# DeltaNet norms by 32-column sums and 32-row spreads, and adaLN units of a spot summed in one bank

## What is computed

```python
mod = silu(c) @ ada_w[l] + ada_b[l]          # once for the context's c_ctx, once for the latents' c
h = rmsnorm(x, norms[0]) * (1 + scale1) + shift1
z = h @ w_in                                 # attention, gMLP and DeltaNet inputs, gates
q = l2norm(silu(short_conv(q))) * DK ** -0.5 # l2norm(x) = x * rsqrt(sum(x * x) + EPS), 4 heads of DK = 128
k = l2norm(silu(short_conv(k)))
merged = g_a * (o_a @ wb[0]) + g_b * (o_b @ wb[1]) + g_c * (o_c @ wb[2])
x = x + gate1 * rmsnorm(merged @ w_out, norms[1])
h2 = rmsnorm(x, norms[2]) * (1 + scale2) + shift2
x = x + gate2 * rmsnorm(ffn(h2), norms[3])   # layer 0: dense SwiGLU; layer 1: top 2 of 8 experts
```

## Time and profile before

| | before |
|---|---|
| median of 3 runs | 2011.56 us (2010.69 to 2015.3) |
| the profiled execution's own time | 2011.39 us |
| its span, first to last instruction | 2009.5 us |
| PE busy | 1895.5 us (94%) |
| PE weight loads busy (beside PE) | 1658.8 us (83%) |
| DVE busy | 1174.5 us (58%) |
| ACT busy | 948.3 us (47%) |
| POOL busy | 264.2 us (13%) |
| DMA | 386.13 MB, mean 192 GB/s |

### The profile page before, as it was taken

One profiled execution on the slowest core, in us unless ns is written; L12 is line 12 of the kernel. 1 busy time (PEld: TensorE's weight loads), 2 busy tenths in 40 slices (PEclk: granted clock), 3 DMA queues, 4 the chain that ended last, 5 costly groups with the idle time before them and its releaser, 6 DMA issues.

```text
span 2009.5 us, 33463 instructions
## 1 busy us (share of the span) xinstructions
PE 1895.5 (94%) x14064; PEld 1658.8 (83%) x14064; DVE 1174.5 (58%) x1383; ACT 948.3 (47%) x1205; POOL 264.2 (13%) x237
## 2 busy tenths in 40 slices
PE   4999899999989999999998999999989999999995
PEld 2889688888868999878987898888868888888884
DVE  1955435454644344338763444546458888888885
ACT  2444622223435222224445322225357888877874
POOL 2510033132000000005300323320010000000001
PEclk9999889999988999999998899999989999999997
DMA  9461142124543333346611322226469999999994
GB/s 343 169 221 50 41 185 69 44 85 146 191 172 111 126 125 126 126 146 230 232 57 43 148 69 81 71 100 209 165 221 384 383 381 379 382 381 381 380 380 158
DMA packets 205556, 386.13 MB, mean 192 GB/s; under 512 B 5609, under 2 KB 65025, under 8 KB 204928
## 3 DMA queue, kind: packets, MB, share of 16 engines
q1 hardware_dynamic: 202048, 371.73, 51.8%
q0 software_dynamic: 3392, 12.70, 1.8%
HBM read 355.05 MB, written 29.36 MB: 191 GB/s over the span
## 4 chain that ended last, share of the span: by engine, by line
PE 84%; DMA 5%; ACT 4%; DVE 4%; issue 1%; POOL 0%; SPq 0%; POOLq 0%; DVEq 0%; ACTq 0%
PE bank L1490 8%; PE bank L1493 8%; PE bank L1491 8%; PE bank L969 6%; PE bank L1198 4%; PE bank L971 4%; PE bank L970 4%; PE bank L1381 3%; PE bank L1379 3%; PE bank L1380 3%; PE bank L1005 3%; PE bank L1007 3%; PE bank L1006 3%; DMA ring<-in_w_in 2%; PE bank L902 2%; PE bank L1334 2%
## 5 line engine op out<-in xcount | busy, mean ns | idle before, releaser
L1542 ACT ACTIVATE ring_split<-ring 128x1024 fp32r<-128x1024 f32 (+2 forms) x84 | 119.4, 1439 | 178.4 <-DMA ring<-in_ffn_w_up 103.8
L971 PE MATMUL bank<-hT_hi,ring_split 128*128 128x384 f32 x576 | 197.5, 343 | 0.0
L630 DVE TENSOR_TENSOR ring_split<-ring,w_upper_a 128x1536 fp32r<-128x1536 f32 (+2 forms) x90 | 161.5, 1816 | 22.0 <-ACT w_upper_a L625 21.5
L630 DVE TENSOR_TENSOR ring_split<-ring,w_upper_b 128x2048 fp32r<-128x2048 f32 (+1 forms) x80 | 155.6, 1956 | 26.1 <-ACT w_upper_b L625 25.9
L2343 DVE TENSOR_TENSOR ring_split<-ring,ring_split 128x2048 fp32r<-128x2048 f32 (+1 forms) x28 | 73.9, 2671 | 142.3 <-ACT ring_split L1542 142.3
L1491 PE MATMUL bank<-ring_split,xg_hi 128*128 128x512 f32 (+1 forms) x400 | 152.0, 380 | 0.0
L625 ACT ACTIVATE w_upper_a<-ring 128x1536 fp32r<-128x1536 f32 (+2 forms) x90 | 136.1, 1535 | 25.3 <-PE bank L1493 25.0
L969 PE MATMUL bank<-hT_hi,ring_split 128*128 128x384 f32 x384 | 143.9, 375 | 4.3 <-DVE modv L2017 2.9
L625 ACT ACTIVATE w_upper_b<-ring 128x2048 fp32r<-128x2048 f32 (+1 forms) x80 | 130.3, 1643 | 15.4 <-PE bank L1493 13.3
L1007 PE MATMUL bank<-ring_split,hT_hi 128*128 128x256 f32 x480 | 136.5, 284 | 0.0
L970 PE MATMUL bank<-hT_lo,ring_split 128*128 128x384 f32 x384 | 131.9, 344 | 0.0
(11 more groups left out here) (396 smaller groups left out, 4816.6 us busy)
## 6 DMA issues: line engine op xcount, KB each, us to landing
ring<-in_w_in SPq DMA_DIRECT2D x28, 2048.0 KB, 9.3
ring<-in_ada_w SPq DMA_DIRECT2D x24, 2048.0 KB, 12.8
ring<-in_moe_w_gate SPq DMA_DIRECT2D x40, 1024.0 KB, 7.2
ring<-in_moe_w_up SPq DMA_DIRECT2D x40, 1024.0 KB, 9.4
ring<-in_moe_w_down SPq DMA_DIRECT2D x20, 1536.0 KB, 10.6
ring<-in_moe_w_down SPq DMA_DIRECT2D x10, 1280.0 KB, 9.7
oT<-in_moe_w_down SPq DMA_DIRECT2D x10, 1280.0 KB, 7.2
ring<-in_w_branch SPq DMA_DIRECT2D x8, 1536.0 KB, 12.8
```

The source lines that it names most:

```text
L630: op.tensor_tensor(m_half(m_place(j, True), j, h), m_half(m_place(j), j, h), m_half(w_upper[j % 2], j, h).bitcast(F32), ALU.subtract).then ...
L971: last = mm(out, lo, hT_hi[:, k], start=False, stop=k == KT - 1)
```

## The change

It has two parts. First, the row sums of q and k are eight products with 32 columns of ones, each into its own group of 32 rows of bank 2 (q) or bank 3 (k), and none accumulates. ACT takes two square roots of 128x388 (the scale DK of q moves from the selector to the activation), DVE one reciprocal of 128x776, and a spread reads the 32 rows of its head's group (K = 32). Second, the units of a spot form a set, which accumulates in one bank: a wider `scP` puts unit c of a set into rows 2c and 2c+1 of each group. A set has one copy, one turn (with 2 columns for each unit) and one take. There are 12 sets, so 12 turns, copies and takes instead of 24. Some places move as well: the quads of `wo` stand before the wait for the merge and its turn behind the gain rows; the turn of `nb` stands behind the transposes; and that of `n4` between the halves of layer 1's transposes.

```diff
 def ada_quad(n, half, b):
-    u = at_ring("ada", n)
-    b = ada_bank(n, b)
+    u, s = at_ring("ada", n), ADA_SET[n]
+    c, c_last = n - ADA_SETS[s][0], len(ADA_SETS[s]) - 1
     if half == 0:
         arrived(u)
-        if n >= 2:
-            pe.wait_ge(ada_cp, n - 1)
+        if c == 0 and s:
+            pe.wait_ge(ada_cp, s)
     for j in range(ADA_G):
         k = ADA_G * half + j
-        last = mm(B[b][ADA_M * j:ADA_M * (j + 1), :], scP[:, k], wslot(u, KT, 512)[:, k],
-                  start=half == 0, stop=half == 1)
+        last = mm(B[b][ADA_M * j:ADA_M * (j + 1), :], scP[:, k, ADA_W - 2 - 2 * c:ADA_W - 2 - 2 * c + ADA_M],
+                  wslot(u, KT, 512)[:, k], start=half == 0 and c == 0, stop=half == 1 and c == c_last)
...
+def ada_turn(units, b, buf):
+    w = 2 * len(units)
+    pe.wait_ge(ada_ev, set_end(units))
     for m in range(4):
-        last = mm(B[b][:, 2 * m:2 * m + 2], ada_rows(n, buf)[:, m * P:(m + 1) * P], ada_sel, start=True, stop=True)
+        last = mm(B[b][:, w * m:w * (m + 1)], buf[:, m * P:(m + 1) * P], ada_sel[:, 0:w], start=True, stop=True)
...
-def turn_x(layer, idx):
+def turn_x(layer, idx, between=None):
     for k in range(KT):
+        if k == 4 and between:
+            between()
...
+    else:
+        turn_x(layer, 0, lambda: ada_turn(ADA_AT[0]["n4"], 7, ada_buf))
...
-                        elif n == P_AT[q] + 1:
-                            ada_turn(u, 2, KK_)
+                        elif n == P_AT[q] + 1 and u == at["p"][-1]:
+                            ada_turn(at["p"], 2, KK_)
...
 def row_sums():
-    for j in range(8):
-        last = mm(B[2][0:8, 0:COUT], rowsel[j // 4][:, 7 - j:15 - j], dsq[:, j], start=j == 0, stop=j == 7)
+    for i in range(2):
+        for h in range(DNH):
+            last = mm(B[2 + i][HQ[h], 0:COUT], ones[:, 0:32], dsq[:, DNH * i + h], start=True, stop=True)
...
                 for j in range(8):
                     if j >= 3:
                         wait(pe, "qkn", layer, j - 1)
-                    mm(B[(2, 3, 7)[j % 3]][:, 0:COUT], ident[0:8, j:j + 1].to_broadcast([8, P]), dsq[0:8, 0],
+                    r = HQ[j % DNH]
+                    mm(B[(2, 3, 7)[j % 3]][:, 0:COUT], ident[r, r.start:r.start + 1].to_broadcast([32, P]), dsq[r, j // DNH],
                        start=True, stop=True).then_inc(S["dst"], 1)
...
+                ada_quads(at["wo"], 0)
+                pe.wait_ge(mod_ok, 4 * layer + 2)
                 wait(pe, "br_ev", layer, 7)
-                ada_units(at["wo"], 2, ada_buf)
-                pe.wait_ge(ada_cp, at["wo"][-1] + 1)
-                pe.wait_ge(mod_ok, 4 * layer + 2)
                 for half in range(2):
                     gain_row(layer, 2, 0, half, 2 + half)
+                ada_turn(at["wo"], 0, ada_buf)
...
-                ada_units(at["nb"], 2, ada_buf)
-                pe.wait_ge(ada_cp, at["nb"][-1] + 1)
+                wait(pe, "xk", layer, 2)
+                ada_quads(at["nb"], 7)
                 turn_x(layer, 1)
+                ada_turn(at["nb"], 7, ada_buf)
...
                 if at["n4"]:
-                    ada_units(at["n4"], 2, ada_buf)
-                    pe.wait_ge(ada_cp, at["n4"][-1] + 1)
+                    wait(pe, "xk", layer, NT + 2)
+                    ada_quads(at["n4"], 7)
...
-                go(dsq[0:8, 0], B[2][0:8, 0:COUT], ACT.Sqrt, bias=l2eps[0:8]).then_inc(S["droot"], 1)
+                go(dsq[:, 0], B[2][:, 0:COUT], ACT.Sqrt, bias=eps128, scale=float(DK))
+                go(dsq[:, 1], B[3][:, 0:COUT], ACT.Sqrt, bias=eps1).then_inc(S["droot"], 1)
...
-                for n in at["wo"][:1]:
-                    ada_copy(n, 2, ada_buf)
                 split_merged(7)
+                ada_copy(at["wo"], 0, ada_buf)
                 split_out("w18b")
-                for n in at["wo"][1:]:
-                    ada_copy(n, 2, ada_buf)
...
-                v.reciprocal(dsq[0:8, 0], dsq[0:8, 0]).then_inc(S["qkn"], 1)
+                v.reciprocal(dsq[:, 0:2], dsq[:, 0:2]).then_inc(S["qkn"], 1)
```

More of the change, by code:

```diff
@@ L81 @@
 ADA_M, ADA_G = 32, 4
+ADA_SETS = [ADA_FIRST] + [at[spot] for at in ADA_AT for spot in ("p", "d0", "d1", "oc", "wo", "nb", "n4") if at[spot]]
+ADA_SET = {n: i for i, units in enumerate(ADA_SETS) for n in units}
+ADA_W = 2 * max(len(units) for units in ADA_SETS)
 ADA_DONE = {3: (1, 0), 5: (2, 1), 9: (4, 2), 11: (5, 3)}
@@ L348, in build, with set_end @@
         grow, gjunk = v3(ring[:, SLOT:SLOT + 2 * D], 2), ring[:, 2 * SLOT:2 * SLOT + D]
[L350 to L356, removed]
+        def set_end(units):
+            return ADA_SET[units[-1]] + 1
         off = [0]
@@ L1303, in _ @@
                 token_tiles(layer, T_Z, 13)
-                for n in at["oc"]:
-                    for half in range(2):
-                        ada_quad(n, half, 6)
+                ada_quads(at["oc"], 6)
                 for t in range(NT):
@@ L1311, in _ @@
                     last.then_inc(S["oc_mm"], 1)
-                for n in at["oc"]:
-                    ada_turn(n, 6, KK_)
+                ada_turn(at["oc"], 6, KK_)
                 wait(pe, "oc_ev", layer, 3)
@@ L1545, in _ @@
             act.wait_ge(sc_zero, 1)
-            go(scP[:, :, 0:2], rows[:, 160:176].rearrange("p (s k) -> p k s", s=2), ACT.Silu).then_inc(sc_ok, 1)
+            go(scP[:, :, ADA_W - 2:ADA_W], rows[:, 160:176].rearrange("p (s k) -> p k s", s=2), ACT.Silu).then_inc(sc_ok, 1)
             def y_root(layer, idx, t):
@@ L1755, in _ @@
                     gates_of(pair, "head")
-                    for n in at[("d0", "d1")[pair]] if pair < 2 else ():
-                        ada_copy(n, 0, dn_rows)
+                    if pair < 2 and at[("d0", "d1")[pair]]:
+                        ada_copy(at[("d0", "d1")[pair]], 0, dn_rows)
                     for x in range(2):
@@ L1784, in _ @@
                     evac(T_Z + t, zs[:, t], ACT.Silu)
-                for n in at["oc"]:
-                    ada_copy(n, 6, KK_)
+                ada_copy(at["oc"], 6, KK_)
                 for t in range(NT):
@@ L1883, in _ @@
                     x_root(1, 0, 1)
-                    for n in at["n4"]:
-                        ada_copy(n, 2, ada_buf)
+                    ada_copy(at["n4"], 7, ada_buf)
                     x_root(1, 0, 2)
@@ L2071, in _ @@
                         x_diag(layer, 0, t)
-                    for n in ADA_FIRST:
-                        ada_take(n, 0)
+                    ada_take(ADA_FIRST, 0)
                 lower_block(0, 0)
@@ L2200, in _ @@
                     lower_gates(splits_by(pair, "head"))
-                    for n in at[("d0", "d1")[pair]] if pair < 2 else ():
-                        ada_take(n, 0)
+                    if pair < 2 and at[("d0", "d1")[pair]]:
+                        ada_take(at[("d0", "d1")[pair]], 0)
                     wait(dve, "d_x", layer, 3 * pair + 3)
```

109 lines of the change are left out of this document (49 added, 60 removed).

## The result

The changed kernel took 1989.18 us (median of 4 runs, 1985.62 to 1996.74), beside 2012.95 us for the kernel before in the same comparison: ratio 0.988, 95% interval 0.9862 to 0.9898, so 21 to 28 us less. Forecast were 14.3 us less and a range from 1990.0 up. The direction was right, the size was not.

The account below looks back on a forecast made before the run. PE was taken to bound the kernel, with shifts passing undiminished to the end. Gains and losses summed to 14.3 us off 2011.39, giving 1997.1, or 1997.3 us as a median; 8 in 10 for 1990 to 2006.

Parts of the forecast that it names:

- I leave that as it is: Behind the spreads, PE's half-clock stretch (1.6 us of work lost) stays; if gone in both layers, 3.3 us more gain.
- Row sums: Row sums of q and k: 5.31 us become 1.46 in column groups, gaining 3.85 a layer, 7.7 in both.
- rival 2: Column groups of the sums run one after the other, losing the 7.7 us: 2005.0 us; chance 0.06.
- Reciprocal: Before the spreads, DVE's reciprocal of 776 columns ends at 153.5, covered with 0.6 us to spare; cost 0.
- rival 3: The reciprocal becomes PE's wait before the spreads: 1998.3 us at 8 ns a column, 2001.5 at 10; chance 0.15.
- Spreads: Spreads overlap until DVE's multiplies set the pace: 5.54 to 4.2 us, gaining 1.3 a layer, 2.5 in both.
- Rival 1: Spreads do not overlap, so 2.5 us less gain: 1999.8 us; chance 0.17.
- wo, layer 0: Quads fill PE's idle stretch before the merge; products start 5.5 us earlier, less 1.1 for slow stretches: 4.4 gained.
- n4: The turn between layer 1's transposes makes modulation late by 2 to 3.3 us; taken as a 3.3 us loss.
- rival 4: n4 costs more, 5 to 6 us: 1999 to 2000 us; chance 0.15.
- nb: Turn moved behind the transposes: 0.6 us gained in layer 0, 0.8 lost in layer 1.
- Rival 5: Slower than before through the clock, with twelve or more extra half-clock stretches (2016 us); chance 0.04.

Follow-up runs that it names:

- inplace_twice: The changed kernel with pooled sets at their old places and the turns of wo, nb and n4 issued twice each: 2000.19 us, ratio 0.9922.
- wo_late: The changed kernel with the quads of wo behind the wait for the merge again: 1988.8 us, ratio 0.986 to the kernel before the change.
- before_again: The kernel before the change, measured once more with no edit: 2017.55 us, ratio 1.0002.
- after_fourth: The changed kernel, unedited, measured a fourth time as reference on a third chip: 1984.76 us, ratio 0.9859 to the kernel before the change.

## Why the prediction was wrong

The means of two profiles of before and four of after, stage by stage, in us:

| part | forecast | length | of it clock-free |
|---|---|---|---|
| to the end of layer 0's feature tiles | −1.6 | −3.2 | (start waits for data) |
| sums, both layers | −7.7 | −7.7 | −7.7 |
| spreads alone, both layers | −2.5 | −4.3 | −1.7 |
| tiles behind the spreads, both layers | 0 | −0.7 | +0.1 |
| DeltaNet, both layers | 0 | −6.0 | +0.1 |
| wo, layer 0, to w_out's last product | −4.4 | −2.8 | −2.0 |
| nb, layer 0 | −0.6 | −3.9 | −0.6 |
| FFN, layer 0 | 0 | +0.7 | +0.7 |
| n4 | +3.3 | +1.7 | +1.8 |
| feature tiles, layer 1 | −0.8 | −2.3 | −1.4 |
| wo, layer 1 | −0.8 | −2.0 | −1.2 |
| nb, layer 1 | +0.8 | −0.4 | +0.3 |
| whole, to PE's last product | −14.3 | −31 | about −15 |

The −15 is 11.5 beyond layer 0's feature tiles and the 3.2 of length up to their end. Up to there after lost 4 us more than before to half clock and was no longer for it; with this loss taken out as well the sum would be −18.9.

**The step that failed** is the one behind the spreads and in wo: "I leave that as it is", with 3.3 us as the bound for the clock. Beyond the feature tiles of layer 0 PE lost 49 us to half clock in the profiles of before and 33 in those of after, 16 less. Over the executions, the share at half clock was 67 us of 2015.6 before and 53 of 1988.2 after; by this estimate the 27 us between these means are 14 of clock and 13 of work and waits. The forecast of the latter, 14.3, was close by luck, with errors that cancel. I had read the clock's stretches in one execution and thought only of one more or one less, and of a rival in which there would be more; the loss at nb (4.6 us, in each profile with the old code) could be seen in part in the 8.25 us that the 48 transposes took the earlier trace rows where those at the start of layer 1 took 7.25.

So the term that failed is the clock, put at nothing behind the spreads and at a cost of 1.1 us in wo; what the runs showed is about 14 us less of it, which comes with the pooled units.

Where the 16 us lie: nb of layer 0 3.3, wo, n4, feature tiles and nb of layer 1 together 3.3, spreads with the tiles behind them 3.4, and 6 in the two DeltaNets, whose code the change does not touch. With two profiles against four, and 5 to 13 us in one DeltaNet from one execution to the next, these last are not explained, and the other profiles speak for chance: the two DeltaNets together lost 16.7 to 24.9 us (mean 21.6) in the seven of other kernels with pooled units, as much as in the three without (17.8 to 24.4, mean 21.8). What repeats lies outside: beyond layer 0's feature tiles and without the DeltaNets the three profiles with the units apart lost 20.8, 30.3 and 21.2 us, those with sets 10.2 to 16.8, and only inplace_twice 30.0. That is 9 to 10 us; where the rest of the 14 that the mean clock tells of lies is open.

**Row sums**: right, to 0.1 us; rival 2 fell, and the drain that the Trainium skill names (TensorEngine Tiling (Array Packing), Key Properties) is not to be seen: eight products of 388 columns, with the change of mode on both sides, took 1.44 us, where the quad's row had given 1.46. **Reciprocal**: no wait, 0.64 us to spare for 0.6; rival 3 fell. **Spreads**: the mechanism was right, the size was not. DVE's pace and PE's first three left 0.8 a layer where I had 1.3. The first multiply starts 1.05 us behind the first spread and the next tile 0.94 behind the end of the fifth multiply (152.84 + 5 × 0.53), 2.0 together, where I had 1.4: two products of 0.5, though the sums of before show 0.66 for one of 388 columns, and 0.4 for hand-overs. Rival 1 fell by 0.5 us a layer only. **wo, layer 0**: the start of the products right to 0.3 us; the cause that I gave, the filled idle time, gave 1.1 of it (wo_late) and the turn's place 3.5, most of that clock, and w_out's products then took 2.5 us more at the lower clock (37.4 against 34.9, means of four and two profiles) where I had taken off 1.1. **n4**: the lateness was over-sized. Modulation came 1.08 us after ACT could have used it, since ACT also waits for w_in's data (2.39 us in after, where it had waited 1.45); rival 4 fell. **nb**: −0.6 clock-free as forecast, and the clock on top. **Rival 5** had the right quantity and the wrong sign. **Range**: two bounds do not come out of their terms. Spreads without hand-over time gain 1.7 a layer and not 1.5, and the bad ends add up to about 2007 and not 2003; neither touches the lower end, which the result passed.

## What to carry to other kernels

Before costing an edit in a kernel that PE bounds, take the loss to half clock stage by stage, from more than one profile, and the mean clock from many executions: here pooling small units brought back as much clock as all removed instructions and waits gave. Which kind of stretch brings the clock down was not settled: doubling the tiny products seemed to, an idle stretch alone (wo_late) did not. Small fp32 products with few output rows cost their columns, so four of them in column groups cost one, also between full-width products. And before filling an idle stretch, follow what ends it: at wo the merge did, and the filled time gave a quarter of what it seemed to or less.

## What the runs showed of the hardware

- One kernel's executions differ by 10 to 20 us (before: 2003.68 to 2023.19), and the granted clock goes along with it: after took 1985.62 us at 0.974 and 1996.74 at 0.970.
- A DVE reciprocal of 776 columns on 128 partitions took 5.00 us, one of 388 on 8 partitions 2.57: 6.4 and 6.6 ns a column.
- A turn with 6 columns in each product took as long as one with 2 (0.80 and 0.81 us).
- Windows over the unchanged DeltaNet of layer 1, before_again and after_fourth:

```profile
1072.58:1373.14 300.56, 284.86 (x3398) 252.39 (x3397) 134.24 (x228) 104.08 (x211) 74.36 (x77) 0.96 0.26 92
```
```profile
1039.33:1334.72 295.39, 279.83 (x3390) 248.06 (x3389) 134.06 (x227) 103.49 (x210) 74.34 (x77) 0.98 0.27 93
```

The same work takes 5.2 us less at a mean clock of 0.98 than at 0.96.
